# An eighth place for raw gate and up tiles of the experts, and later free times for the tiles behind them

## What is computed

```python
for e in range(N_EXPERTS):                                   # 16 experts
    hidden = jax.nn.silu(t @ w_gate[e]) * (t @ w_up[e])      # 1024 -> 256, twice
    y = y + gate[:, e:e + 1] * (hidden @ w_down[e])          # 256 -> 1024
```

```python
bias = rpb[:, dr[:, None, :, None], dc[None, :, None, :]]    # neighbourhood attention
s_loc = q . k * scale + bias
```

## Time and profile before

| What | us |
|---|---|
| Median of 3 runs | 1558.8 (1557.78 to 1561.91) |
| The profiled execution | 1563.16 |
| Its span, first to last instruction | 1561.4 |
| PE busy in it | 1510.3 (97%) |
| DVE busy | 886.4 |
| ACT busy | 709.1 |
| Expert passes, in the span | 329.1 to 512.4 |

### The profile page before, as it was taken

One profiled execution on the slowest core, in us unless ns is written; L12 is line 12 of the kernel. 1 busy time (PEld: TensorE's weight loads), 2 busy tenths in 40 slices (PEclk: granted clock), 3 DMA queues, 4 the chain that ended last, 5 costly groups with the idle time before them and its releaser, 6 DMA issues.

```text
span 1561.4 us, 23591 instructions
## 1 busy us (share of the span) xinstructions
PE 1510.3 (97%) x9895; PEld 1273.7 (82%) x9895; DVE 886.4 (57%) x1249; ACT 709.1 (45%) x1069; POOL 134.8 (9%) x157
## 2 busy tenths in 40 slices
PE   8999999999999999989999999999999998999998
PEld 6986997978887788645778888888878966899998
DVE  5633656567777769778363332333247858555554
ACT  5526553346665454567333212212236447453434
POOL 3002000010000136200300000000002400000000
PEclk9999999999999999889999999999999999999999
DMA  9478558599998352500623323323263350555552
GB/s 309 142 250 260 162 188 267 181 284 275 275 294 286 82 188 82 162 1 3 133 82 108 108 85 104 106 83 101 76 183 127 109 162 1 162 176 177 188 175 68
DMA packets 228946, 242.28 MB, mean 155 GB/s; under 512 B 13097, under 2 KB 222473, under 8 KB 228713
## 3 DMA queue, kind: packets, MB, share of 16 engines
q1 hardware_dynamic: 226704, 238.19, 47.5%
q0 software_dynamic: 1600, 2.37, 2.3%
q10 hardware_dynamic: 536, 0.22, 0.1%
HBM read 239.71 MB, written 1.05 MB: 154 GB/s over the span
## 4 chain that ended last, share of the span: by engine, by line
PE 87%; DVE 6%; ACT 3%; DMA 2%; issue 1%; SPq 1%; DVEq 0%; ACTq 0%
PE bank L813 18%; PE bank L814 18%; PE bank L815 18%; PE score_banks L1341 3%; PE bank L1998 2%; PE bank L2005 2%; PE bank L1375 2%; PE bank L2001 2%; PE bank L912 1%; DVE small L1416 1%; PE bank L913 1%; PE bank L914 1%; PE bank L1358 1%; PE score_banks L947 1%; PE bank L839 1%
## 5 line engine op out<-in xcount | busy, mean ns | idle before, releaser
L802 DVE TENSOR_TENSOR w_lo<-raw,w_hi 128x2048 fp32r<-128x2048 f32 (+1 forms) x143 | 324.9, 2273 | 215.4 <-ACT w_hi L790 214.5
L813 PE MATMUL bank<-xn_hi,w_hi 128*128 128x256 f32 (+1 forms) x1216 | 401.4, 330 | 1.9 <-DVE w_lo L802 0.8
L815 PE MATMUL bank<-xn_hi,w_lo 128*128 128x256 f32 (+1 forms) x1216 | 398.4, 328 | 0.0
L814 PE MATMUL bank<-xn_lo,w_hi 128*128 128x256 f32 (+1 forms) x1216 | 398.4, 328 | 0.0
L790 ACT ACTIVATE w_hi<-raw 128x2048 fp32r<-128x2048 f32 (+1 forms) x143 | 269.7, 1886 | 126.7 <-PE bank L815 76.8
L813 PEld LDWEIGHTS bank<-xn_hi,w_hi 128*128 128x128 f32 x1216 | 231.2, 190 | 23.9 <-issue 1.8
L815 PEld LDWEIGHTS bank<-xn_hi,w_lo 128*128 128x128 f32 x1216 | 231.2, 190 | 20.1
L814 PEld LDWEIGHTS bank<-xn_lo,w_hi 128*128 128x128 f32 x1216 | 231.2, 190 | 19.8
L1845 DVE SCALAR_TENSOR_TENSOR xT<-bank,mod,xT 128x256 f32<-128x256 f32 x96 | 40.6, 478 | 119.7 <-PE bank L815 97.9
L813 PE MATMUL bank<-hid_hi,w_hi 128*128 128x256 f32 (+1 forms) x328 | 107.7, 328 | 0.6 <-DVE hid_lo L1106 0.6
L814 PE MATMUL bank<-hid_lo,w_hi 128*128 128x256 f32 (+1 forms) x328 | 106.8, 326 | 0.0
(11 more groups left out here) (468 smaller groups left out, 2662.8 us busy)
## 6 DMA issues: line engine op xcount, KB each, us to landing
raw<-in_w_ada SPq DMA_DIRECT2D x48, 1024.0 KB, 5.8
raw<-in_w_in SPq DMA_DIRECT2D x30, 1024.0 KB, 6.5
raw<-in_w_gate SPq DMA_DIRECT2D x22, 1024.0 KB, 5.4
raw<-in_w_up SPq DMA_DIRECT2D x22, 1024.0 KB, 5.4
raw<-in_w_exp_down SPq DMA_DIRECT2D x16, 1024.0 KB, 8.6
raw<-in_w_down SPq DMA_DIRECT2D x16, 1024.0 KB, 5.3
raw<-in_w_out SPq DMA_DIRECT2D x12, 1024.0 KB, 5.7
raw<-in_w_exp_up SPq DMA_DIRECT2D x12, 1024.0 KB, 9.0
```

Source lines behind the costliest of these rows:

```text
L802: dve.tensor_tensor(w_lo[:, raw_slot[r], 0:k * cols], raw[:, raw_slot[r], 0:k * cols], high_half(name).bitcast(F32), ALU.subtract)\
L813: pe.matmul(o, s_hi, m_hi, start=i == 0, stop=False)
L814: pe.matmul(o, s_hi, m_lo, start=False, stop=False)
L815: last = pe.matmul(o, s_lo, m_hi, start=False, stop=i == n - 1)
```

## The change

An eighth place, slot 7, is added for gate and up tiles: its raw part is `sq`, its low part a view `aux_lo` over `aux`. The estimate for tiles behind the experts is raised by two passes, so that the planner counts their places as free two passes later. POOL can no longer load the bias table during the experts, since `aux` may hold a low part: the 16 waits for the passes are replaced by one wait for the gate and up products of the last pass, and the 16 loads follow it in one go.

```diff
-MORE_SLOTS = 2
+MORE_SLOTS = 3
@@ leaves(r)
-        return r - first_expert - 1 if r < first_expert else len(PASSES) + r - last_expert
+        return r - first_expert - 1 if r < first_expert else len(PASSES) + 2 + r - last_expert
@@ buffers
+        room = nc.sbuf_tensor("aux_lo", [P, KC, S], F32R)
+        aux_lo = room.__enter__()
+        room.__exit__(None, None, None)
         aux = sb("aux", [P, KC, S])
@@ more_slot(slot)
             i = slot - RAW_SLOTS
+            if i == 2:
+                return sq[:, :, :], aux_lo[:, :, :]
@@ POOL, the loads of the bias table
-                            if l == 0:
-                                pool.wait_ge(*dve_misc.at(("expert gated", 4 * h + r)))
+                            if l == h == r == 0:
+                                pool.wait_ge(*tile_used.at(("pair", len(PASSES) - 1)))
```

## The result

| | before | after |
|---|---|---|
| Median of 22 runs each, us | 1561.89 | 1567.49 |
| Ratio after / before | | 1.0033, 95% interval 1.0022 to 1.0044 |
| The profiled execution, us | 1563.16 | 1566.8 |
| Its span, us | 1561.4 | 1565.1 |

The ratio is +5.2 us (0.0033 x 1562), the profiled executions differ by 3.7 us in their spans. The forecast was 4.8 us less; the side that came is rival C. The forecast of 1554.0 us stood on the median of 3 runs, 1558.8; the 22 runs have 1561.89. So of the 13.5 us between 1554.0 and 1567.49, 3.1 are the base, and 10.4 the way from the forecast -4.8 to the measured difference of the medians, +5.6. In the kernel after, these lines of code stand five lower than before (L1998 is L2003, L947 is L952, L2741 is L2746); a run that adds lines of its own moves them further.

The account below looks back on a forecast made before the run. PE, busy 97% of the span, was taken as the bound. Stop -3.4, lower clock -1.7, side-by-side chunks +0.3 gave -4.8 off the 1558.8 median: 1554.0 us; own range 1551.0 to 1556.0, 8-in-10 range 1551.0 to 1560.0.

Parts of the forecast that it names:

- rival C: Behind the experts: the bias burst goes ahead of the `ada` loads, PE stands 6 to 12 us; 1561.9 to 1567.7; chance 0.08.
- The cost of the stop: At pass 17 PE stands 3.43 us waiting for up 13, then runs at half clock, losing 1.7; together 5.1 us.
- the common view: Experts 8 and 14 lose it, one pass each; their chunks then run side by side: +0.3 us on PE.
- Part 2: Side-by-side chunks for experts 8 and 14: 0.017 us a chunk, 16 chunks, +0.3 us on PE's path.
- Part 1: Eighth place: up 13 issued near 457.1, landing at 467.9; the stop at pass 17 goes, -3.4 and -1.7 us.
- rival A: The stop moves on to pass 18 or 19 because the DMA engines are the limit; 1556.7 us; chance 0.12.
- Part 3: Raised free times behind the experts: every tile there waits for the same former tenant as before; 0 us.
- Part 4: Bias loads leave the passes, return as a burst at about 506.8 beside the `ada` loads; taken as hidden, 0 us.
- the cover of 6.9 us: Behind the experts: time from the `ada` loads' landing at 516.0 to PE wanting them at 522.89.
- the even share: Burst and `ada` loads share the DMA engines evenly: 6 us become 12, landing near 522 at the worst.
- B: Gain smaller without the profiler: 1555.7 us without the clock term, 1557.4 with half the stop, 1556 given; chance 0.15.
- D: Up 13 is held by the rule of three loads, not its place, so the stop stays; 1559.1 us; chance 0.05.

Follow-up runs that it names:

- run 4: The kernel of run 2 plus 16 extra, unread bias loads during the passes, as the kernel before had them: 1558.1 us, ratio 0.9971.
- run 3: Kernel before, seven places, with layer 0's 16 bias loads in one burst held until the second `ada` load landed: 1557.39 us, ratio 0.9965.
- run 7: Kernel before, bias loads left in the passes but reading 1024-byte rows (table not the reference's): 1557.97 us, ratio 0.9969.
- run 6: The kernel of run 2 without the two passes added to the planner's estimate for tiles behind the experts: 1571.34 us, ratio 1.0054.
- run 2: Kernel after, with the burst of bias loads held until the second `ada` load has landed: 1559.43 us, ratio 0.9971.
- run 1: Kernel before, seven places, with layer 0's 16 bias loads in one burst behind the last pass's gate and up products: 1565.73 us, ratio 1.0017.

## Why the prediction failed, step by step

**The cost of the stop: right.** 5.1 us for the stand and the clock, 0.3 back for the common view; the scatter starts 4.9 us earlier, and run 4 gives 0.29% or 4.5 us in timed runs (the interval is 2.3 to 6.6). L2004 (now L2009) has 24 matmuls instead of 40, the 16 fewer that Part 2 counted; their 0.3 us was not measured by itself.

**Part 1: right in its times, incomplete in its cause.** Up 13 was to be issued at 457.1 and was at 457.23. With the bias loads left in the passes (run 4) it landed at 467.9, to the tenth as worked out, which is in part luck; without them at 465.4. Up 14 and 15 were to land by 477.0 and 486.0 and did at 475.2 and 483.9, so rival A did not come. But I had read one row, that the place came free 0.5 us ahead of the issue, as "the place was the limit". The load that followed took 10.8 us, where two `ada` loads took 6.3, and to shorten it was just as sufficient. In run 3 it landed at 470.3 and in run 7 at 470.9. The latest landing without a stop, 470.3 in the prediction, is 471.0 and 470.9 there, since up 11's last matmul stands 0.7 and 0.6 us later in these traces (463.10 and 462.94 against 462.39); so in run 7 nothing was to spare. I had counted the engine time of the bias loads and used it only to argue that up 12 would be early. I had also misread its size: the earlier trace rows has 55 packets, more than the 32 of one load, and the queue row of 395:435 has 5.1 us for four loads, not 6 for five.

**Part 3: right against the kernel before, where nothing moved;** run 6 shows what it protects from.

**Part 4: the step that failed.** It says: "If the two kinds share evenly, the loads' 6 us of engine time become 12, landing near 522 at the worst. I take 0." The load came 14.0 us later than before (20.3 against 6.3), twice the cover of 6.9 us. Rival C had the mechanism, the place and nearly the price: its 13.1 us from layer 1's burst against 14.0 measured, its +7.9 at the low end against 8.8 in the profile and 9.7 in the timed runs. So every number was in the text; the choice between them was wrong. I chose by a stretch of 40 us with one bias load in each pass, and said of it that "neither kind stood behind the other". That row is a mean over time and says nothing of what a queue of 16 does to a load beside it. Cut finer, the same trace says the opposite. In 424:430 there is one bias load, beside a weight load that was issued at 423.13; for two us the weights all but stop, at a full DMA share. The kernel before in 425:427, run 3 in 425:427, then q0 of the kernel before in 424:430:

```profile
425.00:427.00 2.00, 2.00 (x12) 1.62 (x11) 1.97 (x1) 1.04 (x3) 0.00 (x0) 1.00 0.97 77
425.00:427.00 2.00, 2.00 (x12) 1.64 (x11) 1.85 (x2) 1.04 (x3) 0.00 (x0) 1.00 1.08 397
q0 software_dynamic: 32, 0.07, 38.6%
```

The row that was like the new place was the earlier trace rows, and there the engines were taken for 65.3% of 20 us.

How far the two kinds were from even sharing is to be seen at 508:512 in the kernel after: a DMA share of 0.95 and 33 GB/s, where the earlier trace rows have 382 GB/s at 1.05. Its queues in that stretch:

```profile
DMA packets 64, 0.13 MB, mean 33 GB/s; under 512 B 32, under 2 KB 32, under 8 KB 64
q0 software_dynamic: 64, 0.13, 94.9%
```

All 64 packets are the burst's, and none of the weights' started. In the row of 500:526, 512 packets of q0 took 47.9% and 3813 of q1 34.4% of the engines: 0.39 us a packet (0.479 x 26 x 16 / 512) against 0.038 us (0.344 x 26 x 16 / 3813), ten to one on the mean of unlike packets. So equal turns would not have been equal time, which is what I had taken them for. The DMA: Bandwidth & Descriptors page of the Trainium skill says, in its section SWDGE vs HWDGE vs iDMA, that an engine takes turns between the software and the hardware queue, and its section Queues, rings and completion order adds that a turn is a whole packet. The stretch of 508:512 does not show such turns, 64 packets to none. SP's own issues stood at the same time (19.07 us for four), so it may be that its queue had nothing to offer; whether it was that, or that the engines took no turns, no run here decides.

**Rivals B and D.** B, a smaller gain without the profiler: runs 2 and 4 both give 4.5 us, and their intervals (2.5 to 6.7 and 2.3 to 6.6) leave out half a stop, which is a gain of 1.4, but not a stop without the clock term, which is 3.1. So B is not borne out, nor wholly excluded. D is excluded by the issue at 457.23.

**The chances.** C had 0.08 for a price of 14 us against a cover of 7. Of three readings of that price two (13.1 and 18.9) lay beyond the cover and only the even share inside, and that one no row showed.

## What to carry to other kernels

When small scattered loads are gathered into a burst, price them by the engines' time in a row where such a burst stands, not by their bytes and not by a mean over a long stretch, and compare that with the cover of the next load that someone waits for. A mean over 40 us hid here that the weights stood for two us behind a single such load. Before a buffer is added because a load is issued late, look at how long that load takes once it is issued: if it is slow, find out what held up the loads ahead of it, for a cheaper change may be to take that away; here the 16 bias loads moved behind the `ada` loads (run 3) did as much as an eighth place, a new plan and the same move (run 2). A burst that nobody needs soon belongs behind the last load that somebody does.

## What the runs showed of the hardware

- 64 KB read in rows of 256 bytes took 1.3 us of all 16 DMA engines in the passes (12.7% of 40 us, 4 loads); in rows of 1024 bytes 0.22 us (2.2%), for the same bytes and as many packets. The DMA: Bandwidth & Descriptors page of the Trainium skill, in its section Specifications, gives 512 bytes as the least for the full rate; the two means stand on either side of it and agree.
- Short rows alone don't fix that price. Single bias loads of the kernel before, of the same form, took 2.3 us of the engines (38.6% of 424:430) and 0.21 us (7.1% of 408:411), each beside weight loads. What tells them apart is open:

```profile
q0 software_dynamic: 32, 0.07, 7.1%
```

- In the burst a load took 0.78 us of the engines (47.9% of 26 us, 16 loads), and with wide rows 0.33.
- Beside such a burst a load of 1024 KB took 20.3, 19.6 and 18.3 us (16, 16 and 8 loads), 11.4 with wide rows, and 5.4 without it. SP's next four issues took 19.07 us in all beside the burst of 16, and 3.50 in run 2: SP itself stood.
- With a wait of PE of 6.1 us in the kernel after, the clock was at its lower level from 523.7 to 530.5, until 5.3 us behind the end of the wait (0.52 and 0.50 in the rows of the kernel after). In run 1, with a wait of 5.4 us, it was low in one row of 3.4 us, and 0.97 in the next:

```profile
524.50:527.90 3.40, 2.89 (x19) 1.42 (x19) 0.35 (x1) 0.85 (x3) 1.75 (x2) 0.52 0.43 93
527.90:531.30 3.40, 3.40 (x16) 2.82 (x15) 3.06 (x1) 0.52 (x2) 3.40 (x1) 0.97 0.66 137
```

Open: why the weights stand for some five us near the start of a burst, of eight loads or of sixteen, whether because the engines take the burst's packets first or because SP's queue is held up; and why like bias loads take the engines for anything from 0.21 to 2.3 us.
